# Two transformer blocks on one core: an FFN's output product finished bank by bank, with the half rows added and measured as their bank completes

## The reference, cut to what matters

```python
# first stack, l = 0, 1
x = x + 0.5 * swiglu(rms_norm(x, ffn1_norm[l]), w_gate, w_up, w_down)
x = x + hybrid_mixer(rms_norm(x, mix_norm[l]), ...)
x = x + 0.5 * swiglu(rms_norm(x, ffn2_norm[l]), w_gate, w_up, w_down)
x = rms_norm(x, final_norm)        # once, after l = 1
# second stack, l = 0, 1
x = _layernorm(DEEPNORM_ALPHA * x + FFN_RES * _swiglu(x, ffn1_w_in[l], ffn1_w_out[l]), ln1_g[l], ln1_b[l])
x = _layernorm(DEEPNORM_ALPHA * x + _hybrid_mixer(x, ...), ln2_g[l], ln2_b[l])
x = _layernorm(DEEPNORM_ALPHA * x + FFN_RES * _swiglu(x, ffn2_w_in[l], ffn2_w_out[l]), ln3_g[l], ln3_b[l])
```

## Time and profile before

| | us |
|---|---|
| median of 3 runs | 2876.13 (2874.94 to 2878.03) |
| the profiled execution, its own time | 2875.68 |
| its span, first to last instruction | 2873.8 |
| PE busy in the span | 2831.5 (99%) |
| DVE busy | 1817.9 (63%) |
| ACT busy | 1485.6 (52%) |
| POOL busy | 231.6 (8%) |

### The profile page before, as it was taken

How to read it: one execution, slowest core, us unless ns; L and a number is a source line. 1 busy time by engine, 2 the same in 40 slices (tenths; PEclk the granted TensorE clock), 3 DMA queues, 4 the chain that set the end, 5 groups by cost and what they waited for, 6 DMA issues and landing times.

```text
span 2873.8 us, 45049 instructions
## 1 busy us (share of the span) xinstructions
PE 2831.5 (99%) x18180; PEld 2515.9 (88%) x18180; DVE 1817.9 (63%) x2698; ACT 1485.6 (52%) x2304; POOL 231.6 (8%) x187
## 2 busy tenths in 40 slices
PE   8999999999999999999999999999999999999998
PEld 8989878989989879989988887899799888878897
DVE  5646665646655675645568778665555587786654
ACT  5445555445445555444446567544344465675442
POOL 0010001010010011010014100010100131000100
PEclk9999999999999999999999999999999999999999
DMA  6544444555544445555555444555555454444553
GB/s 237 180 168 162 145 154 176 178 180 191 199 163 141 147 153 197 193 193 194 189 178 178 144 154 147 205 198 183 184 197 191 171 194 138 163 148 181 204 201 117
DMA packets 74780, 504.11 MB, mean 175 GB/s; under 512 B 8752, under 2 KB 10448, under 8 KB 18768
## 3 DMA queue, kind: packets, MB, share of 16 engines
q1 hardware_dynamic: 74576, 501.24, 49.1%
HBM read 500.12 MB, written 1.08 MB: 174 GB/s over the span
## 4 chain that ended last, share of the span: by engine, by line
PE 83%; DVE 9%; ACT 4%; issue 1%; POOL 1%; DMA 0%; SPq 0%; DVEq 0%; ACTq 0%
PE ps L1485 41%; PE ps L1503 37%; PE ps L1524 2%; DVE wlo L1945 2%; DVE conv L2240 1%; DVE pr L2342 1%; ACT whi L1681 1%; POOL wlo L2402 1%; PE ps L1611 1%; ACT pr L1910 1%; DVE sm L2343 1%; DVE pr L2339 1%; ACT pr L1916 1%; ACT pr L1908 1%; PE ps L1609 1%
## 5 line engine op out<-in xcount | busy, mean ns | idle before, releaser
L1681 ACT ACTIVATE whi<-raw 128x1024 fp32r<-128x1024 f32 (+3 forms) x938 | 976.9, 1043 | 878.3 <-PE ps L1485 443.6
L1945 DVE TENSOR_TENSOR wlo<-raw,whi 128x1024 fp32r<-128x1024 f32 (+2 forms) x894 | 1076.1, 1216 | 301.4 <-ACT whi L1681 300.4
L1503 PE MATMUL ps<-xT_hi,whi 128*128 128x256 f32 x3296 | 926.9, 281 | 1.0 <-DVE v_mla L2167 1.0
L1503 PE MATMUL ps<-xT_lo,whi 128*128 128x256 f32 x3296 | 920.4, 279 | 0.0
L1503 PE MATMUL ps<-xT_hi,wlo 128*128 128x256 f32 x3296 | 919.8, 279 | 0.0
L1503 PEld LDWEIGHTS ps<-xT_hi,whi 128*128 128x128 f32 x3296 | 619.4, 188 | 7.9 <-issue 6.9
L1503 PEld LDWEIGHTS ps<-xT_lo,whi 128*128 128x128 f32 x3296 | 619.6, 188 | 0.6
L1503 PEld LDWEIGHTS ps<-xT_hi,wlo 128*128 128x128 f32 x3296 | 619.4, 188 | 0.0
L1485 PE MATMUL ps<-whi,xT_hi 128*128 128x512 f32 (+2 forms) x1152 | 462.7, 402 | 6.8 <-DVE wlo L1945 2.4
L1485 PE MATMUL ps<-whi,xT_lo 128*128 128x512 f32 (+2 forms) x1152 | 449.6, 390 | 0.0
L1485 PE MATMUL ps<-wlo,xT_hi 128*128 128x512 f32 (+2 forms) x1152 | 449.3, 390 | 0.0
(11 more groups left out here) (315 smaller groups left out, 2482.2 us busy)
## 6 DMA issues: line engine op xcount, KB each, us to landing
raw<-in_w SPq DMA_DIRECT2D x436, 1024.0 KB, 4.8
vr<-in_vrows SPq DMA_DIRECT2D x19, 512.0 KB, 5.7
raw<-in_w SPq DMA_DIRECT2D x12, 768.0 KB, 4.2
raw<-in_w SPq DMA_DIRECT2D x10, 896.0 KB, 4.5
sums<-scratch SPq DMA_DIRECT2D x8, 512.0 KB, 4.6
raw<-in_w SPq DMA_DIRECT2D x4, 832.0 KB, 4.5
raw<-in_w SPq DMA_DIRECT2D x4, 576.0 KB, 3.7
x<-in_x SPq DMA_DIRECT2D x2, 512.0 KB, 5.3
```

Of the source, the lines that this page charges most:

```text
L1503: made = e.matmul(out, ws[:, o:o + 128], xs[:, kt, :], start=kt == 0 and n == 0 and c % 2 == 0, stop=kt == job.nk - 1 and n == 2, skip_gro ...
L1681: e.activation(out, raw, ACT.Copy).then_inc(*mark("hi", i))
L1945: e.tensor_tensor(out, raw, hi.bitcast(F32), sub).then_inc(*mark("lo", i))
```

## The change

The last two pieces of a down product, L-1 and L, are no longer multiplied piece by piece with both banks in each. For each row half t both pieces go into bank 0 first and then both into bank 1. When bank 0 is complete, its half row is added at once (`add_x` for one n), and where a layer norm follows, its moments (`moments`, a `bn_stats`, taken out of `layernorm`) are taken at once. The same for bank 1. In the mixer's output product, which already made one bank at a time, only the moments move: they follow each half row's addition. The counts of matmuls, additions, moments, splits and DMAs stay as they are.

```diff
-    def rows(self, i, t, job):
-        self.do("rows", i, t, job, self.lo_of[i], [job.xt.ready[kt][t] for _, kt, _ in self.pieces[i][2]])
...
+    def rows(self, i, t, job, banks=(0, 1)):
+
+        self.do("rows", i, t, job, self.lo_of[i], [job.xt.ready[kt][t] for _, kt, _ in self.pieces[i][2]], banks)
...
         if late:
-            for j in range(late):
+            whole = late - 2 if half else late
+            for j in range(whole):
                 if pre and j == late - 1:
                     pre()
                 i = self.take(key, j)
                 self.rows(i, 0, job)
                 done[0] = ("mm", i, 0)
+            if half:
+                for n in (0, 1):
+                    for j in (whole, whole + 1):
+                        i = self.take(key, j)
+                        self.rows(i, 0, job, (n,))
+                    done[0] = ("mm", i, 0) if n else ("mm", i, 0, 0)
+                    half(0, n, done[0])
             if post:
                 self.relieve()
             mid(done[0])
-            for j in range(late):
+            for j in range(whole):
                 if post and j == late - 1:
                     post()
                 i = self.take(key)
                 self.rows(i, 1, job)
                 done[1] = ("mm", i, 1)
+                self.done()
+            if half:
+                for n in (0, 1):
+                    for j in (0, 1):
+                        i = self.take(key, j)
+                        self.rows(i, 1, job, (n,))
+                    if n == 0:
+                        post()
+                        half(1, 0, ("mm", i, 1, 0))
+                done[1] = ("mm", i, 1)
+                self.done()
                 self.done()
...
+        st = [self.stat(12) for _ in (0, 1)]
+        self.row_half = lambda t, n, bank, there: self.do("moments", e, t, n, there, bank, st[t])
...
-        def update(t, tok):
-            self.do("add_x", s, t, (0, 1), banks[t], 0.5, tok, self.x_free[t], in_psum)
+        def half(t, n, tok):
+            self.do("add_x", s, t, n, banks[t][n], 0.5, tok, self.x_free[t], in_psum)
+            self.row_half(t, n, banks[t][n], ("xnew", s, t, n))
...
         self.fence = (toks[1],)
         for f in turned:
             f()
         self.catch_up()
-        self.second = update(1, toks[1])
+        half(1, 1, toks[1])
+        self.second = new(1)
...
-    def layernorm(en, t, halves, banks, st, mv, ve, r, lg, tg, lb, tb):
+    def layernorm(en, t, banks, st, mv, ve, r, lg, tg, lb, tb):
         for n in (0, 1):
-            dve.wait_ge(*at(*halves[n]))
-            made = e.bn_stats(st[:, 6 * n:6 * n + 6], banks[n][:, :])
-        step(made)
+            dve.wait_ge(*at("vec", "moments", en, t, n))
...
+    def moments(en, t, n, there, bank, st):
+        dve.wait_ge(*at(*there))
+        e.bn_stats(st[:, 6 * n:6 * n + 6], bank[:, :]).then_inc(*mark("vec", "moments", en, t, n))
```

More of the change, by code:

```diff
@@ L451, in one, with gemm @@
         return [a], [f, f]
[L453 to L456 removed]
+    def rows(self, i, t, job, banks=(0, 1)):
+        self.do("rows", i, t, job, self.lo_of[i], [job.xt.ready[kt][t] for _, kt, _ in self.pieces[i][2]], banks)
+    def gemm(self, key, xt, nk, outs, free, mid=None, pre=None, post=None, half=None):
         job = Job(xt, nk, outs, free)
@@ L612, in enter_ln @@
         (lg, ig, tg), (lb, ib, tb) = self.vrow(g), self.vrow(b)
+        st = [self.stat(12) for _ in (0, 1)]
+        self.row_half = lambda t, n, bank, there: self.do("moments", e, t, n, there, bank, st[t])
         def f(t, halves, banks):
-            self.do("layernorm", e, t, halves, banks, self.stat(12), self.stat(2), self.stat(1), self.stat(1),
-                    lg, tg, lb, tb)
+            if t:
+                self.row_half = lambda *_: None
+            self.do("layernorm", e, t, banks, st[t], self.stat(2), self.stat(1), self.stat(1), lg, tg, lb, tb)
             for i in (ig, ib):
@@ L706, in ffn, with new @@
         turned = []
-        def update(t, tok):
-            self.do("add_x", s, t, (0, 1), banks[t], 0.5, tok, self.x_free[t], in_psum)
+        def half(t, n, tok):
+            self.do("add_x", s, t, n, banks[t][n], 0.5, tok, self.x_free[t], in_psum)
+            self.row_half(t, n, banks[t][n], ("xnew", s, t, n))
             if not in_psum:
-                for n in (0, 1):
-                    self.main.put(banks[t][n], ("xnew", s, t, n))
+                self.main.put(banks[t][n], ("xnew", s, t, n))
+        def new(t):
             return then(t, [("xnew", s, t, n) for n in (0, 1)], banks[t])
@@ L721, in ffn @@
                          [(*n01[0], *n01[1]), (*n23[0], *n23[1])],
-                         lambda tok: turned.extend(update(0, tok)), post=post)
+                         lambda tok: turned.extend(new(0)), post=post, half=half)
         self.fence = (toks[1],)
@@ L737, in update @@
             def update(t, tok):
-                self.do("add_x", s, t, (n,), [banks[t]], half, tok, self.x_free[t], in_psum)
+                self.do("add_x", s, t, n, banks[t], half, tok, self.x_free[t], in_psum)
+                self.row_half(t, n, banks[t], ("xnew", s, t, n))
                 rows[t].append(banks[t])
@@ L1471, in tensor_program, with rows @@
     pieces, ident = plan(), m["ident"]
-    def rows(i, t, job, lo_there, ready):
+    def rows(i, t, job, lo_there, ready, banks):
         _, w, kts = pieces[i]
@@ L1483, in rows @@
             for n, (xs, ws) in enumerate(((job.H, hi), (job.H, lo), (job.L, hi))):
-                for bank, c0, c1 in job.outs[t]:
+                for bank, c0, c1 in [job.outs[t][b] for b in banks if b < len(job.outs[t])]:
                     made = e.matmul(bank[:, 0:c1 - c0], xs[:, kt, sl], ws[:, j * w + c0:j * w + c1],
                                     start=kt == 0 and n == 0, stop=kt == job.nk - 1 and n == 2)
-        made.then_inc(*mark("mm", i, t))
+        made.then_inc(*mark("mm", i, t, *(banks if banks == (0,) else ())))
     def columns(i, job, lo_there, ready):
@@ L2051, in halve_o, with add_x @@
         e.tensor_tensor(xt.L[:, k:k + 2, :], src, xt.H[:, k:k + 2, :].bitcast(F32), sub).then_inc(*mark("xlo", *key))
-    def add_x(s, t, ns, banks, half, tok, x_free, in_psum):
+    def add_x(s, t, n, bank, half, tok, x_free, in_psum):
         dve.wait_ge(*at(*tok))
@@ L2056, in add_x @@
             dve.wait_ge(*at(*f))
[L2057 to L2061, removed]
+        xs = halves_of(m["x"][t])[n]
+        e.scalar_tensor_tensor(out=bank[:, :] if in_psum else xs, in0=bank[:, :], scalar=half, in1=xs, op0=mul, op1=add
+                               ).then_inc(*mark("xnew", s, t, n))
+    def moments(en, t, n, there, bank, st):
+        dve.wait_ge(*at(*there))
+        e.bn_stats(st[:, 6 * n:6 * n + 6], bank[:, :]).then_inc(*mark("vec", "moments", en, t, n))
     def scores(key, ps, sm, sm_free, scale, slope, bias, bias_there, nm):
@@ L2357, in vector_program @@
         "lo": lo, "to_T": to_T, "turn": turn, "turn_h": turn_h, "mean_square": mean_square, "rms": rms,
-        "final": final, "layernorm": layernorm, "alpha": alpha, "silu": silu, "scale_gate": scale_gate, "glu": glu, "halve_h": halve_h, "halve_o": halve_o,
+        "final": final, "moments": moments, "layernorm": layernorm, "alpha": alpha, "silu": silu, "scale_gate": scale_gate, "glu": glu, "halve_h": halve_h, "halve_o": halve_o,
         "add_x": add_x, "scores": scores,
@@ L2382, in mean_square, with layernorm @@
         root(r, ms, en, t)
-    def layernorm(en, t, halves, banks, st, mv, ve, r, *_):
+    def layernorm(en, t, banks, st, mv, ve, r, *_):
         root(r, ve, en, t)
```

1 line of the change is left out of this document (added).

## The result

The changed kernel takes 2887.31 us, the median of 6 runs (2886.76 to 2888.30), against 2876.24 for the kernel before in the same comparison (2874.94 to 2878.03): 11.1 us more, a ratio of 1.0039 [1.0028, 1.0050]. It is slower. The forecast was 2883.3 in a range of 2877.8 to 2887.5, so the direction and the range held, the second only just: the named 2883.3 lies 7.1 us above the same median of the kernel before, and 11.1 were measured. The profiled execution took 2887.28, 11.60 above the profiled one of before.

The account below looks back on a forecast made before the run. PE, busy 99% on unchanged matmuls, bounds the kernel, so only its gaps and the end can move. Terms 4.4 + 1.5 + 0.4 + 2.8 + 0 - 0.8 - 0.65 = +7.65 us on 2875.68 give 2883.3, range 2877.8 to 2887.5.

Parts of the forecast that it names:

- the swap: At junctions A to E GpSimd does t = 1's root before L+4's low half, which PE needs for the next product.
- A: Junction after a down product, twice: PE starts L+4 at 208.0 instead of 205.77, +2.2 us each, +4.4 together.
- B: Junction after a down product: PE's pass over L+4 starts at 651.2 instead of 649.70, +1.5 us.
- C: Junction after a down product: statistic 0.6 us earlier, but L+4 at 1280.3 instead of 1279.94, +0.4 us.
- the end: End of the program: first addition 1.0 us earlier, then four instructions taking 2.9; -0.65 us, bounds -0.4 and -1.2.
- L+4 is there in time: Rival, 10%: GpSimd's swap does not hold PE, only gains of some 6.4 us remain, 2869.3.
- The load into `raw`: Load into the buffer L+4 leaves: starts up to 2 us later, costed at nothing; uncovered, up to 2 us at seven places.
- The statistics: t = 1's statistics at D and E come 1.1 us earlier, bounds 0.6 and 1.4.
- D: Layer-norm junction, twice: all eight t = 1 transposes stand behind L+4's late pass; 1.4 us later each, +2.8 together.
- E: Layer-norm junction: L+4 starts at 2076.2 against 2076.20; the 1.6 us of removed waits eaten by the new one, 0.
- M: Mixer's output product, two junctions: only moments move, 0.6 less 0.2 us at each of two waits of 0.78, -0.8 together.
- What the profile was to name: Sign: GpSimd's `wlo` releases L1514's matmuls, waits about 2.4 us at A, 1.5 at B, 2.1 at D, 1 at E.

Follow-up runs that it names:

- Experiments 1 and 2: 1: changed kernel, `done` back between the last two pieces' second passes, 2871.5 us; 2: kernel before, only L+4's splits moved behind t = 1's root, 2893.45 us.
- experiment 5: Changed kernel with the mixer output product's first half rows' moments emitted behind DVE's weight low half: 2884.41 us, ratio 1.0029.
- experiment 7: Changed kernel with the first four transposes of t = 1 at junction D ahead of the pass over L+4: 2883.12 us, ratio 1.0026.
- experiment 4: Kernel before with only PE's matmul order changed, the last two pieces of each down product bank by bank: 2877.35 us, ratio 1.0006.
- 6: Changed kernel with L+4's splits in their old place and the mixer's first moments later: 2869.53 us, ratio 0.9978.

## Why the prediction was right, and where not

**What held.** PE's list has the same work, and the swap decides. At A the term was 2.2 and measured 2.18: the waits before were 0.24 + 0.80, after it 2.41 + 0.80. B (1.5, measured 1.47), C (0.4, 0.30) and the end (-0.65, -0.6) held too. The forecast's bounds of 2880.9 and 2885.4 can be remade from its terms only to about 0.2 us. Experiments 1 and 2 show the cause from both sides: without the swap the kernel gains 4.6 us, with it alone it loses 17.4. "L+4 is there in time" is refuted: the low half starts at 206.39 at A, where it had to start before 203.5. The load into `raw` that comes later cost nothing that a step shows. At the end, addition to aggregate is 2876.80 to 2879.65, 2.85 us where 2.9 was worked out.

**The statistics came 1.4 us earlier, not 1.1**, the upper bound. At D the remaining chain, addition to aggregate, is 1470.98 to 1472.51, 1.53 us, as costed; but the root moved from 1467.04 to 1472.98 while PE's matmuls ahead of D stood 7.36 later, so 1.42 earlier. That makes E -0.40 where 0 was forecast: its gaps of 0.38 and 1.21 became 0.39 and 0.82. The three waits of 0.38 ahead of t = 0's transposes went, as said; the 0.39 that E shows is t = 1's.

**D's term was mis-sized by the clock.** The mechanism is as put: the wait at L+4 (1.86; 2.1 said), a pass of 1.47 (1.5 said), then 1.32 from the first transpose to the next matmul (1.3 said), from 2273.76, 2275.23 and 2276.55 in experiment 5. With the clock at 1.00 this costs 0.98 to 1.03, which is 1.4 less the 0.3 us by which the statistics came earlier than costed. In the profiled execution each D was followed by 3.4 us at 1.2 GHz: 2.19 and 2.03, some 1.1 more each. The forecast had no term for the clock, though it added waits of up to 2.4 us at places where PE had run through. The trace of the kernel before held a sign of it, in a mixer's branch of the first stack (PE, then the stretch behind that wait, columns as above):

```profile
1058.23 0.63 PE L1524 MATMUL ps<-ident,xn 128*128 128x128 f32 x4 [2.43 <-DVE xn L2183]
...
1058.85:1062.26 3.41, 2.81 (x10) 2.41 (x10) 3.38 (x6) 1.26 (x4) 0.00 (x0) 0.50 0.51 216
```

At the same wait of 2.43 us one layer earlier, up to 427.98, the clock stayed. Over the kernel some 3 us of the 11.6 go with the clock: 1.1 + 1.1 at D, and 0.49 and 0.27 in two mixers' branches, where it stood at 0.50 too (at the second of them before the change also). In the second execution of the changed kernel it fell in neither branch, so these two belong to the execution.

**M's term had the wrong sign.** "Only moments move, no list of pieces changes" was true and not enough: two moments of 0.70 us went ahead of DVE's low half, and it stood close beside GpSimd's. The turn's wait did shrink, from some 0.78 to 0.45 and 0.39, which is the -0.4 of the forecast; but PE lost 0.8 at the low half first. Net +0.5 each instead of -0.4: 1.8 us, the largest miss of the sum that isn't the clock. The numbers read as an exclusive lock. GpSimd first: its low half takes 2.40 (alone 2.38) and DVE's ends at 1883.88, 1.09 after GpSimd's end. DVE first: it takes 1.22, and GpSimd's ends 1870.87 + 2.94 = 1873.81, 2.26 after DVE's end. The Trainium skill, SBUF — State Buffer, section "SBUF: two separate sides", says that of DVE and GpSimd the one that starts first keeps the shared pair of ports for its whole instruction while the other waits; the trace agrees. The forecast had this mechanism, and put it at A alone, where it came as said (DVE's scaling of t = 1's row 2.55 us instead of 0.88, GpSimd 1.94) and cost nothing, ended at 209.01 before PE's pass did. The mechanism was known and priced at the wrong junction.

**What the profile was to name.** Of the new waits I said GpSimd's `wlo` would be their releaser. It is at B; elsewhere the row says "issue". The waits are 2.41 at A, 1.25 at B, 1.86 at D and 0.82 at E, for 2.4, 1.5, 2.1 and 1. The gap and GpSimd's row beside it, not the name, identify it.

**Sum.** Without any fall: 4.4 (A) + 1.5 (B) + 0.3 (C) + 2.0 (D) - 0.4 (E) + 1.0 (M) - 0.6 (end) = 8.2, against 7.65. The falls add 3.0 in the profiled execution; 0.4 is left over at the program's start. In the second and third executions of the changed kernel that step was -0.50 and +0.52, so it belongs to the execution and not to the change. That 8.2 lies so near to 7.65 is in part luck: M came out 1.8 us above its terms, and D 0.8 and E 0.4 below theirs. The falls then took the profiled execution to within 0.2 us of the range's upper end; the second and third executions took 2.4 and 1.4 us less.

**What stays open.** Why one execution falls at A and another at D: the waits are the same to 0.01 us in both, and no run here separates a cause. The losses at A in experiment 7 are not shown to be linked to its gain at D: in the second execution one A fell, not two.

## What to carry to other kernels

When a change alters how often a planner's counter is advanced, read every engine's list around it, not only those of the engines it means to help: here a `done` moved behind both pieces put one low half behind a root and cost more than the whole change could gain. Moving a short instruction ahead of a long SBUF one on DVE can hand the ports to GpSimd, and what was 1.22 us becomes 3.27; look at who starts first on both. And where a change opens gaps of 2 us in a PE that ran through, widen the forecast upwards by about 1 us for each, for what the clock may take behind it: here about half of such waits were followed by a fall.

## What the runs showed of the hardware that was not expected

- The granted clock fell from 2.4 to 1.2 GHz for 3.4 us at waits of PE of 1.86 us and of 2.41 us, and in other executions of the same program did not fall at the same wait. At A and D of the changed kernel and of those of 5 and 7 the fall began between 0.4 us ahead of the end of the wait and 1.5 us behind it. Of these junctions three executions of the changed kernel had it at both D; at both A; at the first A. A fall cost 0.8 to 1.3 us at A and 1.0 to 1.2 at D. In the first stack's mixers, twice in experiment 4 and once in 6, it lasted 6.8 us.
- A low half of DVE, 128x1024 with two inputs in SBUF, took 1.22 us beside a GpSimd low half that began 0.5 us after it, and 3.27 us beside one that began 0.2 us before it. GpSimd's took 2.94 and 2.40.
- One program's time moves with this: 2887.28, 2884.87 and 2885.88 us for three executions of the changed kernel. Of the 2.4 us between the first two, 1.0 arose at the program's start (+0.47 against -0.50); the falls make up the rest (D 2.2 less, A 1.7 more, the two mixers' branches 0.9 less).
